# Second attention: where VectorE divides by the sums within a round

## The reference

```python
# a: differential attention, 4 heads with two maps each, all 528 keys
s = einsum("bqhmd,bkhmd->bhmqk", qb, k) * scale + t5_bias(...)
p = softmax(s); a = p[:, :, 0] - lam * p[:, :, 1]; out = a @ v
# b: neighbourhood attention, 8 heads, 256 keys of the grid and 16 meta keys, with a bias
# c: window attention, 8 heads, 256 or 384 keys and 16 meta keys, with a sink logit per head
m = maximum(max(s), sink); e = exp(s - m); p = e / (sum(e) + exp(sink - m))
```

## Time and profile before

| | us |
|---|---|
| median of 3 runs (2478.31 to 2481.26) | 2481.23 |
| profiled execution, its own time | 2476.59 |
| its span | 2474.6 |
| TensorE busy with matmuls | 2421.6 |
| VectorE busy | 1707.5 |
| ScalarE busy | 1080.8 |
| GpSimd busy | 98.3 |

### The profile page before, as it was taken

One profiled execution on the slowest core, in us unless ns is written; L12 is line 12 of the kernel. 1 busy time (PEld: TensorE's weight loads), 2 busy tenths in 40 slices (PEclk: granted clock), 3 DMA queues, 4 the chain that ended last, 5 costly groups with the idle time before them and its releaser, 6 DMA issues.

```text
span 2474.6 us, 48942 instructions
## 1 busy us (share of the span) xinstructions
PE 2421.6 (98%) x20393; PEld 2228.6 (90%) x20393; DVE 1707.5 (69%) x2951; ACT 1080.8 (44%) x1980; POOL 98.3 (4%) x108
## 2 busy tenths in 40 slices
PE   9999999999999999999999999999989999999998
PEld 7999999996887989898999999898877888989896
DVE  6878775646556979688879585243986445879694
ACT  5444343334434535356535243212874224535252
POOL 0000001000320000001000002000000000000001
PEclk9999999999999999999999999999999999999999
DMA  4233232220001332332232233222112333233332
GB/s 152 84 106 103 101 96 90 80 81 12 4 10 46 104 110 96 111 96 77 83 122 94 97 102 97 71 93 85 52 51 77 98 94 102 95 103 103 103 93 70
DMA packets 72378, 213.00 MB, mean 86 GB/s; under 512 B 12796, under 2 KB 20028, under 8 KB 72032
## 3 DMA queue, kind: packets, MB, share of 16 engines
q1 hardware_dynamic: 70496, 209.03, 26.4%
q0 software_dynamic: 480, 0.73, 0.1%
q10 hardware_dynamic: 1184, 0.12, 0.0%
HBM read 207.61 MB, written 2.20 MB: 85 GB/s over the span
## 4 chain that ended last, share of the span: by engine, by line
PE 84%; DVE 8%; ACT 5%; issue 3%; DMA 0%; DVEq 0%; ACTq 0%
PE PS L866 21%; PE PS L1401 20%; PE PS L1358 11%; PE PS L1360 10%; PE PS L1359 10%; DVE WL L951 2%; ACT WH L939 1%; PE PS L2259 1%; PE PS L1709 1%; PE PS L1708 1%; PE PS L1710 1%; DVE P L2913 1%; ACT P L2879 1%; PE PS L1236 1%; PE PS L2209 1%
## 5 line engine op out<-in xcount | busy, mean ns | idle before, releaser
L1358 PE MATMUL PS<-OPH,WH 128*128 128x256 f32 (+1 forms) x2112 | 603.0, 285 | 7.4 <-ACT TMP L1456 2.7
L1360 PE MATMUL PS<-OPH,WL 128*128 128x256 f32 (+1 forms) x2112 | 600.0, 284 | 0.0
L1359 PE MATMUL PS<-OPL,WH 128*128 128x256 f32 (+1 forms) x2112 | 598.1, 283 | 0.0
L939 ACT ACTIVATE WH<-WR 128x1024 fp32r<-128x1024 f32 (+2 forms) x277 | 275.6, 995 | 564.3 <-PE PS L866 272.9
L951 DVE TENSOR_TENSOR WL<-WR,WH 128x1024 fp32r<-128x1024 f32 (+2 forms) x277 | 318.5, 1150 | 190.5 <-ACT WH L939 190.2
L1358 PEld LDWEIGHTS PS<-OPH,WH 128*128 128x128 f32 x2112 | 401.4, 190 | 11.2 <-DVE OPL L1108 3.2
L1359 PEld LDWEIGHTS PS<-OPL,WH 128*128 128x128 f32 x2112 | 401.2, 190 | 1.1 <-issue 0.7
L1360 PEld LDWEIGHTS PS<-OPH,WL 128*128 128x128 f32 x2112 | 400.5, 190 | 0.0
L939 ACT ACTIVATE WH<-SUMS 128x512 fp32r<-128x512 f32 x352 | 211.0, 623 | 231.3 <-DVE SUMS L977 188.8
L951 DVE TENSOR_TENSOR WL<-SUMS,WH 128x512 fp32r<-128x512 f32 x352 | 234.1, 684 | 21.0 <-ACT WH L939 20.5
L866 PE MATMUL PS<-NHI,WH 128*128 128x264 f32 (+2 forms) x976 | 237.9, 309 | 1.0 <-ACT TMP L2633 1.0
(11 more groups left out here) (475 smaller groups left out, 4610.9 us busy)
## 6 DMA issues: line engine op xcount, KB each, us to landing
WR<-in_ffn_up SPq DMA_DIRECT2D x64, 512.0 KB, 3.9
WR<-in_ffn_down SPq DMA_DIRECT2D x64, 512.0 KB, 3.7
WR<-in_ffn_gate SPq DMA_DIRECT2D x56, 512.0 KB, 3.9
WR_MORE<-in_ffn_gate SPq DMA_DIRECT2D x32, 512.0 KB, 4.5
WR_MORE<-in_ffn_up SPq DMA_DIRECT2D x24, 512.0 KB, 4.1
WR<-in_ffn_down SPq DMA_DIRECT2D x32, 384.0 KB, 3.2
WR<-in_w_gate SPq DMA_DIRECT2D x24, 512.0 KB, 3.6
WR<-in_w_out SPq DMA_DIRECT2D x16, 512.0 KB, 3.6
```

The source lines that it names most:

```text
L939: e.activation(split_unit(i)[0][:, 0:w], src, ACT.Copy).then_inc(S["w_hi"], 1)
L1358: e.matmul(o, wh[:, at:at + 128], hi, start=k == 0 and s in (1, 2, 5), stop=False, skip_group_check=True)
L1359: e.matmul(o, wh[:, at:at + 128], lo, start=False, stop=False, skip_group_check=True)
L1360: last = e.matmul(o, wl[:, at:at + 128], hi, start=False, stop=k == 3, skip_group_check=True)
```

## The change

VectorE's line of the table is written in another order. The entries are the same.

```diff
 STEPS = {"PE": [(3, "turn"), (4, "values"), (0, "scores")],
          "ACT": [(5, "yh"), (3, "pt"), (1, "exp"), (5, "square")],
-         "DVE": [(5, "out"), (5, "yl"), (1, "soft"), (2, "join")]}
+         "DVE": [(5, "out"), (2, "join"), (5, "yl"), (1, "soft")]}
```

## The result

The changed kernel takes 2506.03 us (median of 4 runs, 2503.62 to 2507.54); the kernel before, run beside it, 2480.42 (4 runs, 2478.31 to 2481.26). The ratio is 1.0104 with a 95% interval of 1.0092 to 1.0116: about 25.6 us slower, where +27.4 was forecast.

The account below looks back on a forecast made before the run. VectorE paced the second attention's "a" rounds, a ring of engine waits its "b" and "c" rounds. Adding 18.3 and 9.1 gave +27.4 us: 2504.0 on the profiled execution's scale, median 2508.5, range 2498 to 2520.

Parts of the forecast that it names:

- Term 1: Second attention's 16 "a" rounds: first `soft` to first "b" `soft` grows from 44.85 to 63.2 us, +18.3 us.
- The ring of 3.95 us: "a" rounds: `soft`, `exp`, `join`, next `soft` run without overlap, so a round takes 3.95 us, before 2.86.
- The cover that I named for `pt`: "a" rounds: ScalarE's `pt` (0.65 us) ends before the next `exp` starts; failing that, up to 0.65 us a round.
- Term 2: The 32 "b" and "c" rounds: first "b" `soft` to last `join` grows from 88.7 to 97.8 us, +9.1 us.
- The two waits that I said would come back: "b" and "c" rounds: VectorE's wait for `yh` (10.1 us) and ScalarE's for the transposes (13.3 us) go.
- Releases: Handovers between VectorE and ScalarE: 0.03 to 0.04 us each; at 50 to 100 ns the sum would be 1 to 6 us higher.
- (1): TensorE's idle time in "a" rounds lets its clock fall to 1.2 GHz in spells: about +14, 2522 us; chance 0.08.
- (2): Only the "a" rounds lose; "b" and "c" rounds stay at 5.5 us a pair: +18.3, 2499.5 us; chance 0.07.
- (3): No measurable change: "b" and "c" rounds regain VectorE's 16.6 us of idle time, cancelling the "a" loss: 2483 us; chance 0.04.
- (4): Faster: half the counted wait before "a" `join`, plus VectorE's 16.6 us regained in "b" and "c" rounds: 2474 us; chance 0.03.

Follow-up runs that it names:

- spare copy: One unused 248-column ScalarE copy added between the two exponentials of each "a" unit: 2512.47 us on the changed kernel, 2479.64 us on the kernel before.
- older-join order: Against the kernel before, VectorE's order is `out`, `join` of the unit one older (r-3), `yl`, `soft`: 2488.5 us, ratio 1.0032.
- older join and out: Against the kernel before, `join` (r-3, ahead of `yl` and `soft`) and `out` (r-6) are each of the unit one older: 2477.94 us, ratio 1.0001.

## Why the prediction was right

**Size.** Forecast 2508.5 in a range of 2498 to 2520, measured 2506.03. On the profiled execution's scale the sum gave 2504.0 and it took 2503.62. That it is this close is partly luck: the two stretches grew by 28.1 us against 27.4 forecast, but the stage began 1.5 us earlier in this execution than in that of before (first `soft` at 1724.35 and 1725.86) and what follows it took 0.5 us more.

**Term 1** (+18.3) was +18.6. The ring of 3.95 us for an "a" round came out as 3.95, link by link: `exp` at 1.23 (1.24), its end at 2.79 (2.79), release 0.02 (0.03), `join` 1.14 (1.13). The cover that I named for `pt` holds. Of the range's upper end, 0.65 us a round for `pt` ahead of `exp`, nothing came. One of the 16 intervals is 4.19 us and not 3.95, for which the trace shows no releaser; it makes most of the 0.3 by which the term exceeds the sum. The two runs with the spare copy show that the exponentials are bare in this ring, and were covered before.

**Term 2** (+9.1) was +9.4, and +10.3 in the run that changes only these rounds, 0.9 of it from the round in which the orders meet. The "b" round is 2.58 (2.58), the wide "c" round 3.84 (3.80), the narrow one 3.37 (3.30). Here too the sum is closer than its parts: the sixteen "c" rounds are about 0.9 us longer than forecast together, and the first three rounds, which have `out` in place of `yl`, are 0.7 shorter, which the sum had left out. The two waits that I said would come back did: 0.0 before `yl`, and ScalarE's L2868 next to nothing. The statement on which this term rests, that a round had waited for exp and `yh` and now waits for exp and `join`, is borne out from both sides: `yl` ahead of `join` puts `yh` back on the path and costs more, and `yl` behind `join` in the order of before takes it off and saves 7.7 us of stretch B.

**Releases.** VectorE starts 0.02 us after ScalarE's read ends at 1759.01, and ScalarE some 0.04 after VectorE's. By the 50 to 100 ns of the Trainium skill ("Advanced Engine Details and Errata", section "Network/Comms") the sum would have been up to 6 us higher; the trace, which had been preferred, was right.

**The rivals.** (1) The clock: granted 1.00 from 1740 to 1885 us although TensorE's busy time fell to 39.62 of 49 (some 0.76 us of idle time in a round, where rival 1 had over a microsecond). So nothing like the swing in the Trainium skill's section "A second HAM failure mode: psum-queue depth-cycling" ("TensorE: Matmul & The Clock Gate") occurred here. What did change is that the clock rose later at the stage's start; it put nothing on the rounds that can be seen: the `soft` steps start 3.95 to 3.96 us apart in the part at 1.2 GHz too. The price of rival 1 for a full round at that level stays untested, since the first rounds of the stage lack most of their transposes and products with the values. Its reading of the earlier trace rows was also off: the fall came at 804.2, so the 0.71 of 2.00 us stands mostly behind it; in the 2 us ahead, 802 to 804, TensorE was busy for 0.55. (2) Only the "a" rounds lose: ruled out by the run that changes the others alone, +9.9. (3) and (4) needed a full return of VectorE's idle time in the "b" and "c" rounds; stretch B has more idle time and not less (27.2 of 96 us, before 16.6 of 88). That the return did not come is all that decided against (4). Its other condition, a wait of 1.04 us or less before an "a" `join`, was met by the measured 1.00: the 1.04 is 16.6 divided by 16, a growth of the round at which the sum would be nothing, and was taken for a wait.

**What I had overlooked** touched no number of the forecast but one expectation: VectorE's `out` is a step that can wait too. The prediction counted it as covered, which holds in the changed kernel, where `join` waits longer. In the older-join order that cover is gone, and it cost 8.4 us.

## What to carry to other kernels

These rules are drawn from this one stage. In a hand-pipelined round, where each engine runs its list in order, count for each step what stands between it and the step of the same unit that feeds it through another engine: if that is less than the other engine's time, the round becomes the sum of the ring, whatever the shares of busy time say. Within a round, first do what other engines wait for and what waits for nobody, and last a step whose input comes from the end of another engine's round and for which nobody is in a hurry (here `yl`). Exchanging two neighbours that seem harmless can close a ring: here one copy of 0.28 us, put ahead of `join`, cost 8.4.

## What the runs showed that was not expected

The same added work was free in one order and paid in full in the other: 16 copies of 0.30 us cost stretch A 0.0 and 4.8 us.

The start of the stage wandered from execution to execution, with the same instructions ahead of it: the first `soft` came at 1724.35 us in the changed kernel's profile and at 1733.42 in that of the older join and out, whose span is 2482.0 though its median is that of before. The cause lies ahead of the stage and was not looked for. For changes of some 10 us the stretches of the stage say more than the spans, and they repeat better: A was 44.83 to 44.87 in four kernels with VectorE's old order of the "a" rounds, and B was 88.71 and 88.75 in the two of them that have all of the old order. Each is one profiled execution.
